# Gates for two turns in one load, early rows of v, and coefficients ahead of the sparse sums in the weighing of a PEER layer's v

## The reference, cut to what matters

```python
def peer_layer(h, w_query, peer_keys1, peer_keys2, peer_u, peer_v):
    ...                      # top 16 by two half keys: idx, gates = softmax(scores)
    def chunk_fn(args):
        hx, ix, gx = args
        u = peer_u[ix]
        a = jax.nn.gelu(jnp.einsum('td,thkd->thk', hx, u), approximate=False)
        vsel = peer_v[ix]
        return jnp.einsum('thk,thkd->td', gx * a, vsel)
```

## Time and profile before

| | |
|---|---|
| median of 3 runs | 3449.74 us (3447.45 to 3454.16) |
| the profiled execution | 3451.46 us |
| its span, first to last instruction | 3449.6 us |
| gates' stage and dots, first to last matmul of L797 | 594.6 to 1259.9 us |
| first weighing matmul of L924, start | 1288.9 us |
| last weighing matmul of L924, start | 1833.2 us |
| busy over the span: PE, DVE, ACT, POOL | 83%, 41%, 25%, 28% |

### The profile page before, as it was taken

The page is one execution under the profiler, slowest core; times in us unless marked ns, Lnnn a source line. Parts: engine busy times, 40 slices in busy tenths (PEclk is TensorE's granted clock), DMA queues, the critical chain, the costliest instruction groups (busy, mean ns, idle before and its releaser), DMA issues. The chain is left out here.

```text
span 3449.6 us, 34856 instructions
## 1 busy us (share of the span) xinstructions
PE 2855.9 (83%) x12845; PEld 1978.4 (57%) x12845; DVE 1406.4 (41%) x2394; ACT 854.0 (25%) x1425; POOL 980.9 (28%) x480
## 2 busy tenths in 40 slices
PE   8787667999999969999995946987578888887886
PEld 3565457999999967787774823666322222222322
DVE  0327543995877756555565243432201000000001
ACT  0214221333666633333332201332100000000001
POOL 0012000666877767888871020000000000000000
PEclk9895779999999989999997967557799999999999
DMA  9300121445899999999993120003599999999996
GB/s 354 105 20 4 55 104 38 162 167 182 303 349 346 355 342 327 347 340 342 340 332 115 49 71 13 1 4 129 216 421 421 421 421 421 421 421 421 421 421 280
DMA packets 274707, 862.62 MB, mean 250 GB/s; under 512 B 30487, under 2 KB 118167, under 8 KB 225272
## 3 DMA queue, kind: packets, MB, share of 16 engines
q1 hardware_dynamic: 218136, 697.40, 53.4%
q0 software_dynamic: 38016, 138.43, 10.7%
q10 hardware_dynamic: 18432, 25.17, 2.0%
HBM read 806.38 MB, written 54.53 MB: 250 GB/s over the span
## 5 line engine op out<-in xcount | busy, mean ns | idle before, releaser
L797 PE MATMUL dots_dot_ps<-one_acts,dots_u_split 128*128 128x384 f32 x3072 | 555.8, 338 | 21.8 <-POOL dots_u_split L87 21.2
L924 PE MATMUL val_banks<-val_v,val_coef_split 128*128 128x512 f32 x2304 | 531.6, 391 | 41.8 <-DVE val_coef_split L87 41.2
L797 PEld LDWEIGHTS dots_dot_ps<-one_acts,dots_u_split 128*128 128x128 f32 x3072 | 533.7, 189 | 29.6 <-issue 22.1
L924 PEld LDWEIGHTS val_banks<-val_v,val_coef_split 128*128 128x128 f32 x2304 | 431.0, 188 | 142.4 <-issue 53.9
L87 POOL TENSOR_TENSOR dots_u_split<-dots_u_raw,dots_u_split 128x1024 fp32r<-128x1024 f32 x128 | 332.1, 2595 | 422.9 <-ACT dots_u_split L82 421.9
L87 POOL TENSOR_TENSOR val_v<-val_v_raw,val_v 128x2048 fp32r<-128x2048 f32 x64 | 297.1, 4642 | 82.4 <-ACT val_v L82 82.4
L1482 PE MATMUL moe_up_ps<-all_raw_first,all_xs_t 128*64 128x512 f32 x1152 | 262.6, 597 | 53.3 <-DMA all_raw_first<-in_w_up 31.6
L1549 DVE TENSOR_TENSOR all_x<-moe_y_ps,all_x 128x512 f32<-128x512 f32 x64 | 44.3, 692 | 564.0 <-PE moe_y_ps L1455 564.0
L1482 PE MATMUL moe_up_ps<-moe_raw_more,all_xs_t 128*64 128x512 f32 x896 | 207.8, 604 | 54.5 <-DMA moe_raw_more<-in_w_up 45.6
L888 DVE SCALAR_TENSOR_TENSOR val_banks<-val_v_rows,one_slot_coef,val_banks 128x1024 f32<-128x1024 f32 x128 | 164.4, 1284 | 214.4 <-DMA val_v_rows<-in_peer_v,one_expert 214.3
L1482 PEld LDWEIGHTS moe_up_ps<-all_raw_first,all_xs_t 128*64 128x64 f32 x1152 | 91.2, 136 | 222.0 <-issue 222.0
(11 more groups left out here) (297 smaller groups left out, 3562.9 us busy)
## 6 DMA issues: line engine op xcount, KB each, us to landing
all_raw_first<-in_w_gate SPq DMA_DIRECT2D x80, 1024.0 KB, 23.6
moe_raw_more<-in_w_down SPq DMA_DIRECT2D x80, 1024.0 KB, 24.1
dots_u_raw<-in_u_tiles SPq DMA_DIRECT2D x128, 512.0 KB, 4.3
val_v_raw<-in_peer_v SPq DMA_DIRECT2D x64, 1024.0 KB, 5.0
all_raw_first<-in_w_up SPq DMA_DIRECT2D x64, 1024.0 KB, 25.1
moe_raw_more<-in_w_up SPq DMA_DIRECT2D x64, 1024.0 KB, 25.1
moe_raw_more<-in_w_gate SPq DMA_DIRECT2D x48, 1024.0 KB, 23.6
all_raw_first<-in_w_down SPq DMA_DIRECT2D x48, 1024.0 KB, 25.3
```

Source lines behind the costliest of these rows:

```text
L797: last = self.nc.tensor.matmul(self.banks[:, j, 0:DENSE], self.split[:, j, u_part, k], self.h_t[:, h_part, k, T - DENSE:T], start=(k == 0 ...
L924: last = nc.tensor.matmul(banks[:, 2 * (t + 1) + half, :], coef_split[:, b, c_part, a, t * P:(t + 1) * P], v[:, b, v_part, a, half * BANK: ...
```

## The change

- **A new holder `ValueRows`** places `v_raw`, `dot`, `coef`, `weight` and `part` of the weighing in the tile `shared`, which so lives until the end of the weighing. `v_raw` lies in the first half of `stage`.
- **Rows of v for turns 0 and 1** are issued by SP in the gates' stage, behind the last load of u, when the spans in the first half are stored, and ahead of the rest of span 5's stores.
- **Gates** are read once for two turns: 768 pieces of 1 KB in even turns, none in odd ones, ahead of the dots. Dots and gates have semaphores of their own. SP's loop is written out.
- **VectorE's order** in a turn: low part of the coefficients, products for the next turn, then the two sparse sums of the turn before. The last two sums follow the loop. GpSimd gathers two slots later in its list.
- **The sparse slots of u** are spread over 67 tiles in place of 72.
- The starting credits on the semaphores `v_lo`, `coef_ready` and `coef_lo` go, with the counts shifted.

```diff
@@ -808,23 +808,20 @@
...
-        v_raw = s.sb("v_raw", [P, 2, 2, D])
+        v_raw, dot, weight, coef, part = values.raw, values.dot, values.weight, values.coef, values.part
-        dot = s.sb("dot", [P, 2, 2, DENSE])
-        weight = s.sb("weight", [P, 2, SPANS, 2, SPAN])
-        coef = s.sb("coef", [P, 2, 2, DENSE])
-        part = s.sb("part", [P, 2, BANK])
-        v_loaded = [s.sem(f"v_loaded{i}") for i in range(2)]
-        c_loaded = [s.sem(f"c_loaded{i}") for i in range(2)]
+        v_loaded = values.loaded
+        dot_loaded = [s.sem(f"dot_loaded{i}") for i in range(2)]
+        weight_loaded = [s.sem(f"weight_loaded{i}") for i in range(2)]
@@ -837,18 +834,19 @@
         with nc.Block() as block:
             @block.sync
             def _(sp):
-                def load(turn, b, i):
-                    sp.wait_ge(v_lo, turn + 1)
-                    sp.dma_start(v_raw[:, b], A["peer_v"][bass.ds(turn * (2 * P), 2 * P), :].rearrange(
-                        "(a e) d -> e a d", e=P)).then_inc(v_loaded[b], 16)
-                    sp.wait_ge(coef_ready, turn * 2 + 2)
-                    sp.dma_start(dot[:, b], dots_dram[bass.ds(turn * 2, 2)].rearrange(
-                        "a e t -> e a t")).then_inc(c_loaded[b], 16)
-                    sp.dma_start(weight[:, b].rearrange("p s a t -> p s (a t)"),
-                                 weight_dram[:, :, bass.ds(turn * 2, 2), :].rearrange(
-                                     "s b a t -> b s (a t)")).then_inc(c_loaded[b], 16)
-
-                turns(sp, load)
+                for turn in range(n_turns):
+                    b = turn % 2
+                    if turn >= 2:
+                        sp.wait_ge(v_lo, turn - 1)
+                        values.load_rows(sp, turn, b, turn // 2)
+                        sp.wait_ge(coef_ready, 2 * (turn - 1))
+                    if turn % 2 == 0:
+                        pair = turn // 2
+                        sp.dma_start(weight[:, pair % 2].rearrange("p s a t -> p s (a t)"),
+                                     weight_dram[:, :, 2 * turn:2 * turn + 4, :].rearrange(
+                                         "s b a t -> b s (a t)")).then_inc(weight_loaded[pair % 2], 16)
+                    sp.dma_start(dot[:, b], dots_dram[2 * turn:2 * turn + 2].rearrange(
+                        "a e t -> e a t")).then_inc(dot_loaded[b], 16)
 
             @block.scalar
             def _(act):
@@ -856,28 +854,25 @@
-                    act.wait_ge(coef_ready, turn * 2 + 6)
+                    act.wait_ge(coef_ready, turn * 2 + 2)
-                pool.sem_inc(v_lo, 2)
-                    for c in range(2 * turn + sparse.NR - 2, 2 * turn + sparse.NR):
+                    for c in range(2 * turn + sparse.NR - 4, 2 * turn + sparse.NR - 2):
-                dve.sem_inc(coef_ready, 4)
-                dve.sem_inc(coef_lo, 2)
@@ -889,19 +884,30 @@
                         out=sparse_sum, in0=sparse.rows[:, c % sparse.NR, :], scalar=slot_coef[:, c:c + 1],
                         in1=sparse_sum, op0=ALU.mult, op1=ALU.add).then_inc(sparse.used, 1)
 
-                for turn in range(n_turns):
-                    b = turn % 2
-                    dve.wait_ge(c_loaded[b], 32 * (turn // 2 + 1))
-                    dve.wait_ge(coef_lo, turn + 1)
+                def coefficients(turn):
+                    b, pair = turn % 2, turn // 2
+                    dve.wait_ge(dot_loaded[b], 16 * (turn // 2 + 1))
+                    dve.wait_ge(weight_loaded[pair % 2], 16 * (pair // 2 + 1))
+                    if turn >= 2:
+                        dve.wait_ge(coef_lo, turn - 1)
                     for a in range(2):
                         nc.vector.tensor_tensor(
                             coef[:, b, a].rearrange("p (s t) -> p s t", s=SPANS),
                             dot[:, b, a].rearrange("p (s t) -> p s t", s=SPANS),
-                            weight[:, b, :, a, :], ALU.mult).then_inc(coef_ready, 1)
-                    add_slot(2 * turn)
+                            weight[:, pair % 2, :, 2 * (turn % 2) + a, :], ALU.mult).then_inc(coef_ready, 1)
+
+                coefficients(0)
+                for turn in range(n_turns):
+                    b = turn % 2
                     dve.wait_ge(coef_hi, turn + 1)
                     split_lo(nc.vector, coef_split[:, b, 1], coef[:, b], coef_split[:, b, 0]).then_inc(coef_lo, 1)
-                    add_slot(2 * turn + 1)
+                    if turn + 1 < n_turns:
+                        coefficients(turn + 1)
+                    if turn >= 1:
+                        add_slot(2 * turn - 2)
+                        add_slot(2 * turn - 1)
+                add_slot(P - 2)
+                add_slot(P - 1)
                 step = Steps(dve, dve_step)
                 dve.wait_ge(sparse.used, P)
                 for o in range(8):
@@ -915,8 +921,8 @@
-                    pe.wait_ge(v_lo, turn + 3)
-                    pe.wait_ge(coef_lo, turn + 3)
+                    pe.wait_ge(v_lo, turn + 1)
+                    pe.wait_ge(coef_lo, turn + 1)
@@ -1607,7 +1613,7 @@
-def peer_first_phase(nc, A, ident, dots, shared, score, choice, h_row, expert, slot_coef, weight_dram, gathered):
+def peer_first_phase(nc, A, ident, dots, shared, score, choice, h_row, expert, slot_coef, weight_dram, gathered, values):
@@ -1661,7 +1667,7 @@
-            return range(P * r // LEFT, P * (r + 1) // LEFT)
+            return range(min(P, P * r // (LEFT - 5)), min(P, P * (r + 1) // (LEFT - 5)))
@@ -1684,6 +1690,9 @@
+                sp.wait_ge(stored[0], 16 * PARTS * (SPANS // 2))
+                for turn in range(2):
+                    values.load_rows(sp, turn, turn, 0)
@@ -1871,6 +1880,31 @@
+class ValueRows:
+    def __init__(self, nc, s, A, shared):
+        self.A = A
+        at = 0
+        def room(n):
+            nonlocal at
+            at += n
+            return shared[:, at - n:at]
+        self.raw = room(4 * D).rearrange("p (b a d) -> p b a d", b=2, a=2)
+        self.dot = room(4 * DENSE).rearrange("p (b a t) -> p b a t", b=2, a=2)
+        self.coef = room(4 * DENSE).rearrange("p (b a t) -> p b a t", b=2, a=2)
+        self.weight = room(8 * DENSE).rearrange("p (b s a t) -> p b s a t", b=2, s=SPANS, a=4)
+        self.part = room(2 * BANK).rearrange("p (o n) -> p o n", o=2)
+        self.loaded = [s.sem(f"v_loaded{i}") for i in range(2)]
+    def load_rows(self, sp, turn, b, i):
+        sp.dma_start(self.raw[:, b], self.A["peer_v"][bass.ds(turn * (2 * P), 2 * P), :].rearrange(
+            "(a e) d -> e a d", e=P)).then_inc(self.loaded[b], 16)
@@ -1942,13 +1976,14 @@
+                values = ValueRows(nc, p, A, shared)
-                    peer_first_phase(nc, A, ident, dots, shared, score, choice, h_row, expert, slot_coef, weight_dram, u_gathered)
+                    peer_first_phase(nc, A, ident, dots, shared, score, choice, h_row, expert, slot_coef, weight_dram, u_gathered, values)
-            peer_value_phase(nc, A, dots_dram, weight_dram, x, gate2[:], expert, slot_coef, v_gathered)
+                peer_value_phase(nc, A, dots_dram, weight_dram, x, gate2[:], expert, slot_coef, v_gathered, values)
```

More of the change, by code:

```diff
@@ L808, in activate, with peer_value_phase @@
                       self.gelu[:, j]).then_inc(self.stored[j], 16)
-def peer_value_phase(nc, A, dots_dram, weight_dram, x, gate, expert, slot_coef, gathered):
+def peer_value_phase(nc, A, dots_dram, weight_dram, x, gate, expert, slot_coef, gathered, values):
     DT = DENSE // P
     with Scope(nc, "val") as s:
-        v_raw = s.sb("v_raw", [P, 2, 2, D])
+        v_raw, dot, weight, coef, part = values.raw, values.dot, values.weight, values.coef, values.part
         v = s.sb("v", [P, 2, 2, 2, D], F32R)
-        dot = s.sb("dot", [P, 2, 2, DENSE])
-        weight = s.sb("weight", [P, 2, SPANS, 2, SPAN])
-        coef = s.sb("coef", [P, 2, 2, DENSE])
         coef_split = s.sb("coef_split", [P, 2, 2, 2, DENSE], F32R)
-        part = s.sb("part", [P, 2, BANK])
         sparse = SparseTokens(nc, s, A["peer_v"], expert, "v", gathered)
```

## The result

| | before | after |
|---|---|---|
| median (6 runs each, side by side) | 3453.5 us (3447.45 to 3455.87) | 3498.56 us (3488.58 to 3503.51) |
| ratio, with its 95% interval | | 1.013 (1.0111 to 1.0148) |
| profiled span | 3449.6 | 3497.1 |
| first matmul of the weighing | 1288.90 | 1287.01 |
| first matmul to drain (third output block) | 544.8 | 596.3 |

The change costs 45 us where the forecast was a gain of 20. Of the 47.5 us between the two spans, the head gives back 1.9, the weighing takes 51.5 more, and the rest of the kernel is 2.1 shorter. So the place to read is the weighing, and there first the windows: busy us of PE, PEld, DVE, ACT, POOL, then clock, DMA share and GB/s. They answer to the earlier trace rows.

What follows compares the result with a forecast made beforehand. The prediction took TensorE, at 8.16 us a turn, and the DMA engines as both near their limit in the weighing. Its terms, -20.6 + 8 - 8.3 + 0.5 = -20.4 us, led to a median of 3429.3 us, range 3418 to 3444.

Steps and rivals of the forecast that it cites:

- part 2: Weighing, gates of two turns in one load: 1.5 late even batches expected, +8 us, bounds 0 and 85.
- two in 62: Weighing: rate of late batches assumed in 62 turns, from which 1.5 late ones were taken.
- The price of a miss: Weighing: TensorE delay when a product pair misses its gap before GpSimd's subtraction, 3.1 to 7.6 us, taken as 5.3.
- rival (a): Weighing: four to nine of 32 even batches late, giving 3442 to 3469 us; chance 0.11.
- rival (b): Weighing: packets cost nothing, only bytes count, so half the even turns are late, +85 us or 3506; chance 0.07.
- the two equations on the queues: DMA queues in the weighing: solved for engine cost, a = 0.020 us a packet and b = 34.3 us a MB.
- Part 1, -20.6: Weighing: VectorE's new order puts no sum before a split and removes all stalls, -20.6 us, bounds 0 and 20.6.
- the old stalls: Weighing before the change: 20.6 us of TensorE stalls, blamed on sparse sums awaiting gathered rows and pairs caught behind GpSimd's subtraction.
- The pace of 8.16 us: Weighing: TensorE's own time per turn, read from 33 of 63 pairs of casts of v.
- Part 3, -8.3: Start of the weighing: gates' stage ends at 1267.5, first matmul 13.1 us later, at 1280.6 for 1288.9; -8.3 us.
- the 1 us charged for the moved gathers: Stage of dots: delay from sparse gathers moved forward by spreading slots over 67 tiles, 1 us, between 0 and 9.
- Part 4, +0.5: End of the weighing: four sums instead of two behind the last split, +0.5 us, bounds 0 and 3.

Runs made afterwards that it cites:

- e1: The changed kernel with gates loaded for one turn at a time again, 768 pieces of 512 B in every turn; 3458.3 us.
- e6: e1 with the sparse slots over 72 tiles and all rows of v issued in the weighing, leaving little but VectorE's new order; 3452.29 us.
- e7: The changed kernel with SP issuing a turn's gates and dots before it waits for the free buffer of v; 3427.84 us.
- e11: e7 with gates loaded for one turn at a time in pieces of 512 B; 3432.75 us.
- e12: The kernel before the change, with SP issuing a turn's dots and gates before it waits for the free buffer of v; 3443.51 us.
- e13: e7 with the early rows of v issued behind the last stores of gates instead of ahead of them; 3426.13 us.
- e4: The changed kernel, gates for two turns still issued in even turns, but as two loads in pieces of 512 B; 3492.7 us.

## Why the prediction was wrong

**The step that failed** is in part 2: "so now an even batch is there by some 9.9 + 0.84 = 10.7, with 0.9 us to spare". The 9.9 was the distance at which six turns' pairs began without waiting, and I used it as the time by which a batch has landed. It was no bound: these were among the earliest pairs of the kernel before. The others began up to 13.1 us behind the rows' issue, 10.9 at the median, and so couldn't say whether their data was there at 9.9. Kernels that ask as late as before and load by the turn (e1, e6) show dots at 9.1 to 9.2 us behind their own issue at the median, some 10 behind the rows', and pairs that waited for them 43 times in e1. In the 15 late even batches of the change the pair began as soon as the dots were there, 11.4 to 12.3 us behind the rows' issue (the one shown: 1304.31 to 1315.70), for a forecast of 10.7. The limit was wrong too, on the other side: I let the pair begin until the subtraction does, 11.6 behind the issue. Six of the 15 began inside that limit, the one shown 0.3 us ahead of the subtraction of 1316.00, and were caught, since the pair needs 1.0 itself. The other nine began behind its start, by up to 0.6 us. To end ahead of the subtraction the pair must begin by 10.7, so even by my own landing time there was no room. 15 batches were late, not 1.5. (A sixteenth wait, at 1764.31, met no subtraction and cost nothing.) The wait row of before, three waits for gates with one of 12.5 us, had already shown that the tail reached the limit. I weighed it as two in 62.

**The price of a miss** was 4.8 us where I took 5.3 between 3.1 and 7.6. But it was made otherwise: the stall is the 3.1 of the lower bound (2.95), and the other 1.9 is the clock, which had no term in the sum. Part 2 comes to 15 x 4.8 = 72 us instead of 8. This is rival (a), with 15 late where it went to nine. The time of rival (b), half the even turns late and 3506, was near what came, its reason was not: the two equations on the queues of after, 56119a + 110.05b = 5027 and 17195a + 62.64b = 2536, give a = 0.022 us and b = 34.4 us again, and packets fell by 25.1 thousand (274707 to 249620) for a forecast 24.6. The Trainium skill (DMA: Bandwidth & Descriptors, Specifications) puts line rate at 512 B and above. For the DMA engines' time these rows disagree, though the size of a is less sure than the two equal results make it look: q1 alone, 5408 us before and 5027 after with b held at 34.4, gives 0.014 us a packet. For the kernel's time e7 and e11 agree with the page: with twice the packets of gates the stage was no longer.

**Part 1, -20.6.** In the change itself it can't be seen. With the coefficients early (e7) the stage is 526.5, so 18.3 of the 20.6 were there to be had; the other 2.3 lie outside the 61 distances, at the two ends of the stage. But the new order doesn't get them: e6, with it and without early loads, gets nothing, and the stage of 548.4 is even 3.6 longer in its one profiled execution. In my step "so no sum stands before a split, and each turn can keep 8.16" the first half came true, the second didn't follow. The order that takes the sums away also asks for the dots 1 us sooner behind the issue of the rows (8.9, as e7's pairs begin) than the earliest pair of before (9.9), and they weren't there. The cause of the old stalls, sums that wait for rows ahead of the splits, stands by the evidence of e12 (8.2 us as the rows landed sooner), though not as shown for all 20.6 us. The pace of 8.16 us held; it was the distance of 30 of the 63 pairs of casts, not of 33.

**Part 3, -8.3**, came to -1.9. From first cast to first matmul were 13.7 us for a forecast 13.1. The four gathers came as described, but what GpSimd's subtraction caught was the pair (1279.09, 5.92 us), not the split, so that this term came out nearly right by another way. What was mis-sized is the stage's end: first cast at 1273.29 instead of 1267.5. Two things are late. The last dots were stored at 1265.11 instead of 1261.59, more than the 1 us charged for the moved gathers; 1.6 of the 3.5 us were there at the stage's first matmul already (596.2 for 594.6). And the sparse coefficients were ready at 1266.13, 5 us sooner than before, but for 7 us nothing happened: the stores of gates, which I had given until 1269, were still out. All 48 of them:

```profile
L1684 SPq DMA_DIRECT2D expert_weights<-pe_shared x48: 326/446/974, 936.9 to 1257.3; - x48
...
DMA to landing us min/median/max: 2.9/7.9/15.2
```

The last is issued at 1257.3, and it is the one that took 15.2 us (the same view of 1257.28 to 1257.9 us alone): 1257.3 + 15.2 = 1272.5, 0.8 us ahead of the first cast of v. The kernel before could have shown this: its last two stores of gates, the last issued at 1251.3, took 19.0 us each, until 1270.3, and my 1266.5 had them done by then. Taking the early rows out of their way (e13) brought the first cast to 1268.82. Kernels with an unchanged head differ by 3 us here (1273.29 in the change, 1270.43 in e7), so a part of it is chance.

**Part 4, +0.5**, came out as nothing: the third block followed without a wait.

## What to carry to other kernels

Where one engine issues several loads in turn, put those whose buffers are already free ahead of the one that has to wait: this exchange of two blocks alone was worth 70 us of the stage in the changed kernel and 8 in the old one. When an engine's work is put in a new order, ask what each piece now wants earlier than before. Check a load against the latest time at which its user may begin, and against the spread of its landings, not against turns that happened to start early; where GpSimd's subtraction holds VectorE, a few tenths too late cost the whole subtraction. Even out periodic loads, since two turns' data in one batch leave the sum of bytes as it is and make the worst landing later.

## What the runs showed of the hardware

- TensorE's clock: the stall of 2.96 us was followed by about 3.4 us at granted 0.50, from 1 us behind the restart on, with matmuls of 628 instead of 389 ns, and cost 1.9 us beyond the stall. 14 of the 16 stretches behind a stall show it, with 1.6 to 1.9 us over TensorE's own pace. The two that don't, 0.25 us over, stand behind stalls of 0.92 and of 2.79 us, though two stalls of 2.71 us did bring it.
- A VectorE split that met GpSimd's subtraction was held through a second one that followed at once: 9.72 us in e11 and 9.23 in e1, beside 8.97 and 8.96 of GpSimd. The Trainium skill (SBUF — State Buffer, Who interferes with whom) calls the shared port pair an exclusive lock, which this agrees with; the rows add that here the waiting engine wasn't served between two operations of the other.
- Lateness locked into a cycle: a late batch delays its user but hardly the next issue, so the next batch is in time, and the one after it is late again. The stalls repeat every 37.2 to 37.8 us over most of the stage, and e4, whose batches came hardly later, has the same cycle.
